# Rotary halves on VectorE, and auxiliary steps of a two-layer decoder kernel put in other places, other banks and other sums

## What is computed

```
h = x + 0.5 * rms_norm(swiglu(rms_norm(x), ffn1))
r_q, r_k, r_v, r_g, g_qkv, g_z, g_a, g_b, m_q, gates = split(rms_norm(h) @ w_in)
rotary:  concat([x1 * cos - x2 * sin, x1 * sin + x2 * cos])      # halves of 128 rows, 4 heads of q and of k
o_ret = silu(r_g) * rms_norm(retention(rotary(r_q), rotary(r_k), r_v))
o_gdn = rms_norm(gated_delta(l2(q), l2(k), v)) * silu(g_z)       # q, k, v = silu(short causal convolution of g_qkv)
o_mem = softmax(m_q @ mem_k) @ mem_v                             # 4 heads over 256 memory rows
merged = sigmoid(gates) * (o_ret @ W_ret, o_gdn @ W_gdn, o_mem @ W_mem), summed
h = h + rms_norm(merged @ w_out);  h = h + 0.5 * rms_norm(swiglu(rms_norm(h), ffn2))
```

## Time and profile before

| | |
|---|---|
| median of 3 runs | 1933.48 us (1932.43 to 1934.76) |
| the profiled execution | 1930.05 us |
| its span | 1928.3 us |
| mean granted TensorE clock | 0.99 |
| VectorE, ScalarE, GpSimd busy | 1349.1, 903.6, 120.2 us |
| DMA | 372.48 MB, 193 GB/s |

### The profile page before, as it was taken

The page is one execution under the profiler, slowest core; times in us unless marked ns, Lnnn a source line. Parts: engine busy times, 40 slices in busy tenths (PEclk is TensorE's granted clock), DMA queues, the critical chain, the costliest instruction groups (busy, mean ns, idle before and its releaser), DMA issues. The chain is left out here.

```text
span 1928.3 us, 40625 instructions
## 1 busy us (share of the span) xinstructions
PE 1849.2 (96%) x16354; PEld 1785.9 (93%) x16354; DVE 1349.1 (70%) x2070; ACT 903.6 (47%) x1048; POOL 120.2 (6%) x176
## 2 busy tenths in 40 slices
PE   6999999999998999999999999999999899999997
PEld 6999999988888999999999999998888899999997
DVE  5777577758666867776577756777676776877755
ACT  3533355456654264533354334464566435353433
POOL 0000001101210100000000000110111010000000
PEclk9999999999999999999999999999999999999998
DMA  7676657666764556565667766665666564556653
GB/s 234 187 204 193 182 178 230 213 218 211 253 208 155 180 177 206 164 183 160 182 196 215 200 177 187 214 227 196 232 232 208 166 194 158 175 187 186 185 163 113
DMA packets 436075, 372.48 MB, mean 193 GB/s; under 512 B 9474, under 2 KB 413316, under 8 KB 435010
## 3 DMA queue, kind: packets, MB, share of 16 engines
q1 hardware_dynamic: 411728, 278.76, 48.5%
q0 software_dynamic: 24160, 91.12, 13.6%
HBM read 343.16 MB, written 26.69 MB: 192 GB/s over the span
## 5 line engine op out<-in xcount | busy, mean ns | idle before, releaser
L1715 DVE TENSOR_TENSOR wl<-raw,wh 128x2048 fp32r<-128x2048 f32 (+1 forms) x282 | 603.7, 2141 | 192.3 <-ACT wh L1261 165.5
L1261 ACT CAST wh<-raw 128x2048 fp32r<-128x2048 f32 (+1 forms) x282 | 503.9, 1787 | 250.2 <-PE proj L652 121.7
L652 PE MATMUL proj<-xl,wh 128*128 128x264 f32 x2624 | 380.8, 286 | 0.5 <-DVEq L1846 0.5
L652 PE MATMUL proj<-xh,wh 128*128 128x264 f32 x2624 | 380.7, 288 | 0.0
L652 PE MATMUL proj<-xh,wl 128*128 128x264 f32 x2624 | 371.1, 284 | 2.1 <-DVE wl L1715 2.1
L652 PEld LDWEIGHTS proj<-xl,wh 128*128 128x128 f32 x2624 | 342.0, 189 | 14.1 <-issue 13.2
L652 PEld LDWEIGHTS proj<-xh,wh 128*128 128x128 f32 x2624 | 341.2, 189 | 1.9
L652 PEld LDWEIGHTS proj<-xh,wl 128*128 128x128 f32 x2624 | 339.1, 188 | 3.4 <-DVE wl L1715 3.4
L671 PE MATMUL proj<-hl,wh 128*128 128x264 f32 x704 | 173.3, 283 | 0.0
L670 PE MATMUL proj<-hh,wh 128*128 128x264 f32 x704 | 173.0, 283 | 0.0
L1282 ACT ACTIVATE gate<-gate 128x264 f32<-128x264 f32 x88 | 37.4, 425 | 248.0 <-DVEq L1747 248.0
(11 more groups left out here) (444 smaller groups left out, 2383.0 us busy)
## 6 DMA issues: line engine op xcount, KB each, us to landing
raw<-ffn_w_in SPq DMA_DIRECT2D x176, 512.0 KB, 5.1
raw<-w_in SPq DMA_DIRECT2D x80, 1024.0 KB, 5.6
raw<-ffn_w_out SPq DMA_DIRECT2D x64, 704.0 KB, 4.6
sring<-cache_mem_k POOLq DMA_DIRECT2D x32, 512.0 KB, 5.0
sring<-cache_mem_v POOLq DMA_DIRECT2D x32, 512.0 KB, 4.4
out<-sring POOLq DMA_DIRECT2D x32, 512.0 KB, 4.3
sring<-state_gdn POOLq DMA_DIRECT2D x32, 512.0 KB, 5.4
raw<-w_mem_v SPq DMA_DIRECT2D x10, 1024.0 KB, 6.3
```

The costliest lines, as they stand in the source:

```text
L652: mm = pe.matmul(o, w[:, s, k * 256 + t * P:k * 256 + (t + 1) * P], a[:, k, :], **go)
L1261: act.copy(wh[:, slot, 0:size], raw[:, slot, 0:size]).then_inc(hi_done[slot], 1)
L1715: dve.tensor_sub(wl[:, slot, 0:size], raw[:, slot, 0:size], wh[:, slot, 0:size].bitcast(F32)).then_inc(split_done[slot], 1)
```

## The change

In both layers:

- The swap products and their table are gone. `rotate` makes the swapped halves itself: two VectorE operations of 64 partitions, each reading the other half's partitions, then cosines and sum; the sign moves in the table.
- gq: `rvn0`, `rvn1` from the ends of groups 0 and 1 to the middle and end of group 3, `ro0`, `ro1` to those of group 4, `rst` to the middle of 5, `rvs` from the end of 4 to the middle of 6, `rqd` to the end of 1, `gcs` from the middle to the end of 5. Banks are fixed by `FIRST_BANK` from here to the delta's decays.
- x2: `svt` is turned inside the first half, `rd0` after it, and VectorE takes them in this order; `gct0`, `gct1` one group later; at the end `rS7` comes first, and VectorE updates the state before it reads `gqd` and `rdt`.
- `gvn1` goes from x2's end to rg's first middle, `gkn` from there to the middle of x0's second group, where ScalarE copies it (before: VectorE, 1.22 us).
- The squares are added in pairs by VectorE (`pair_sums`, three operations), so `rn0`, `rn1`, `gm0`, `gm1` take 2 matmuls each and not 4. `rn` goes from the end of rg's group 0 to the middle of group 1. In the decays of the second chunk `gG1` stands before `gbr1`.

```diff
...
-                def rotate(j):
-                    o = begin(l, f"rw{j}")
-                    for t in range(2):
-                        mm = pe.matmul(o[:, t, 0:T], swap[:], rot[:, 2 * j + t, :], start=True, stop=True)
-                    end(mm, f"rw{j}")
...
                     elif g == 3:
+                        ready("rvt")
+                        turn_values(0)
+                    elif g == 4:
                         ready("rvn")
                         outputs(0)
-                    elif g == 4:
+                    elif g == 5:
                         ready("rkd")
                         o = begin(l, "rst")
...
                         end(mm, "rst")
+                    elif g == 6:
+                        turn(l, "rvs", [(j * P, rvt[:, j, SEQ:T]) for j in range(KT)])
...
+                    elif g == 3:
+                        turn_values(1)
+                    elif g == 4:
+                        outputs(1)
                     elif g == 5:
                         pe.wait_ge(scr_loaded, 16 * (l + 1))
                         turn(l, "gcs", [(j * 24, scr[:, j * P:(j + 1) * P]) for j in range(16)])
...
                     if (t, k) == (0, 3):
...
+                        if g:
+                            state_rows(g)
+                        else:
+                            turn_rows("svt", accv, 1)
...
-                        turn_rows("svt", accv, 1)
+                        state_rows(0)
...
-                    if g == 7:
+                    if g == 6:
+                        turn_delta_values(0)
+                    elif g == 7:
+                        update_retention(8)
                         turn_rows("rdt", accr, 2)
                         ready("gprod")
                         o = begin(l, "gqd")
                         end(pe.matmul(o[:, 0, 0:H * NS], ones[:], kneg[:].rearrange("p h b -> p (h b)"), start=True, stop=True), "gqd")
-                    if g in (6, 7):
-                        turn(l, f"gvn{g - 6}", [(j * P, qkvt[:, 8 + j, (g - 6) * P:(g - 5) * P]) for j in range(KT)])
-                    if g == 7:
-                        update_retention(8)
...
                 def turn_keys(g):
                     if g == 0:
-                        ready("gqk")
-                        turn(l, "gkn", [((2 * h + t) * P, qkvt[:, 4 + h, t * P:(t + 1) * P]) for h in range(H) for t in range(2)])
-
-                def finish_retention(g):
-
-                    if g == 0:
-                        ready("rsq")
+                        turn_delta_values(1)
+                    elif g == 1:
+                        second("rsq", 1)
                         for s in range(2):
                             o = begin(l, f"rn{s}")
                             for hd in range(2):
-                                for dt in range(2):
-                                    mm = pe.matmul(o[:, hd, 0:T], ones[:], rsq[:, 4 * s + 2 * hd + dt, :], start=(dt == 0), stop=(dt == 1))
+                                mm = pe.matmul(o[:, hd, 0:T], ones[:], rsq[:, 2 * s + hd, :], start=True, stop=True)
                             end(mm, f"rn{s}")
...
+                        elif g == 1:
+                            turn(l, "gkn", [((2 * h + t) * P, qkvt[:, 4 + h, t * P:(t + 1) * P]) for h in range(H) for t in range(2)])
...
-                        ready("g2sq")
+                        second("g2sq", 1)
...
                             for hd in range(2):
-                                for dt in range(2):
-                                    mm = pe.matmul(o[:, hd, 0:SEQ], ones[:], sqd[:, 4 * s + 2 * hd + dt, :],
-                                                   start=(dt == 0), stop=(dt == 1))
+                                mm = pe.matmul(o[:, hd, 0:SEQ], ones[:], sqd[:, 2 * s + hd, :], start=True, stop=True)
...
                 def rotate(j):
-                    o = take(dve, l, f"rw{j}")[:, :, 0:T]
                     c = 0 if j < 2 else 2
                     r = rot[:, 2 * j:2 * j + 2, :]
+                    for into, other in ((slice(0, HALF_P), slice(HALF_P, P)), (slice(HALF_P, P), slice(0, HALF_P))):
+                        order.apart(tt(sqt[into], r[other], rot_tab[other, c + 1:c + 2, :].broadcast_to([HALF_P, 2, T]), ALU.mult))
+                    order.wait()
                     order(tt(r, r, rot_tab[:, c:c + 1, :].broadcast_to([P, 2, T]), ALU.mult))
-                    order(tt(sqt[:], o, rot_tab[:, c + 1:c + 2, :].broadcast_to([P, 2, T]), ALU.mult))
-                    release(dve, f"rw{j}")
                     order(tt(r, r, sqt[:], ALU.add))
...
-                    if g < NS:
-                        own_part(accr, take(dve, l, f"rd{g}")[:, 0, 0:DV], own_row, g)
-                        release(dve, f"rd{g}")
                     if g == 0:
                         o = take(dve, l, "svt")[:, 0, :]
...
                         tell("o_mem")
-                    elif g == NS - 1:
+                    if g < NS:
+                        own_part(accr, take(dve, l, f"rd{g}")[:, 0, 0:DV], own_row, g)
+                        release(dve, f"rd{g}")
+                    if g == NS - 1:
                         tell("reads")
...
+                def pair_sums(squares):
+
+                    both = squares[:].rearrange("p (h d) t -> p h d t", d=2)
+                    order(tt(squares[:, 0:1, :], squares[:, 0:1, :], squares[:, 1:2, :], ALU.add))
+                    order(tt(squares[:, 1:2, :], squares[:, 2:3, :], squares[:, 3:4, :], ALU.add))
+                    order(tt(squares[:, 2:4, :], both[:, 2:4, 0, :], both[:, 2:4, 1, :], ALU.add))
+
                 def finish_retention(g):
+                    read_delta(g)
                     if g == 0:
-                        order(cp(kn[:].rearrange("p n d -> p (n d)"), flat("gkn")))
-                        release(dve, "gkn")
-                    read_delta(g)
+                        second("rsq", 0)
+                        pair_sums(rsq)
+                        tell("rsq")
...
```

More of the change, by code:

```diff
@@ L21 @@
 AX = mybir.AxisListType
-P = 128
+P, HALF_P = 128, 64
 L = 2
@@ L102 @@
             + " ".join(f"{n}{s}" for n in ("gG", "gQ") + tuple(f"{n}{g}" for n in ("gy", "gt") for g in range(LEVELS)) for s in range(2)) + " " + " ".join(f"{n}{g}" for n in ("gc", "gu") for g in range(SMALL))).split()
-FIRST_BANK = {"rn0": 2}
+FIRST_BANK = {"rn0": 2, **{n: 0 for n in "rkn rs0 rs1 rvn0 rvn1 ro0 ro1 rst rvs".split()}, **{n: 2 for n in "rqd rks gcs".split()},
+              **{f"sv{g}": 3 for g in range(NS)},
+              "spt": 2, "rd7": 2, "rS6": 0, "rS7": 2, "rdt": 0, "gqd": 1, "gvn1": 2, "gd0": 1, "rn1": 0, "gd1": 2, "gbr0": 0, "gG0": 3, "gQ0": 2,
+              "gd2": 0, "gG1": 1, "gbr1": 2, "gQ1": 0}
 PLACE, AUX_USES, AUX_FULL = {}, [0] * 4, [0] * 4
@@ L149, in build @@
         kdec_tab = sb("kdec_tab", [P, 2 * H])
-        ident, swap, tri, ones = (sb(n, [P, P]) for n in ("ident", "swap", "tri", "ones"))
+        ident, tri, ones = (sb(n, [P, P]) for n in ("ident", "tri", "ones"))
         masks = sb("masks", [P, 7, P])
@@ L937, in retention_middle, with turn_values, retention @@
                         end(mm, "rst")
+                    elif g == 6:
+                        turn(l, "rvs", [(j * P, rvt[:, j, SEQ:T]) for j in range(KT)])
+                def turn_values(t):
+                    turn(l, f"rvn{t}", [(j * P, rvt[:, j, t * P:(t + 1) * P]) for j in range(KT)])
+                def retention(g):
+                    if g == 1:
+                        ready("rprod")
+                        o = begin(l, "rqd")
+                        end(pe.matmul(o[:, 0, 0:H * NS], ones[:], kneg[:].rearrange("p h b -> p (h b)"), start=True, stop=True), "rqd")
+                    elif g == 2:
+                        turn(l, "rks", [(h * P, rot[:, 4 + h, SEQ:T]) for h in range(H)])
+                    elif g == 3:
+                        turn_values(1)
+                    elif g == 4:
+                        outputs(1)
                     elif g == 5:
@@ L940, in retention_middle @@
                         turn(l, "gcs", [(j * 24, scr[:, j * P:(j + 1) * P]) for j in range(16)])
[L942 to L957, removed]
                 products(l, "gq", xh, xl, after=retention, mid=retention_middle, inner=values)
@@ L1036, in decays, with key_products @@
                     mats = [(q, 2 * s + q // 2, q % 2) for q in range(4)]
+                    def key_products(step, other):
+                        o = begin(l, f"{step}{s}")
+                        for q, h, c in mats:
+                            mm = pe.matmul(o[:, 0, q * P:(q + 1) * P], qkvt[:, 4 + h, c * P:(c + 1) * P],
+                                           qkvt[:, other + h, c * P:(c + 1) * P], start=True, stop=True)
+                        end(mm, f"{step}{s}")
+                    if s == 0:
+                        ready("gqk")
+                    else:
+                        key_products("gG", 4)
                     o = begin(l, f"gbr{s}")
```

(8 more changed lines are left out.)

138 lines of the change are left out of this document (70 added, 68 removed).

## The result

| | before | changed |
|---|---|---|
| median, 10 runs each | 1932.95 us (1926.45 to 1935.75) | 1938.68 us (1936.89 to 1942.09) |
| ratio to before, 95% interval | | 1.0045 (1.0034 to 1.0055) |
| profiled execution | 1930.05 us | 1936.89 us |

The account below looks back on a forecast made before the run. TensorE, busy 96% of 1928.3 us, was taken as the bound. Gains less waits and clock summed to 2.7 us in layer 1 and 5.3 in layer 0, 8.0 together: 1933.5 - 8.0 = 1925.5 us, 8-in-10 range 1917 to 1932.

Parts of the forecast that it names:

- Rotary: End of rv: VectorE's rotations bound it, TensorE's removed 3.7 us become waiting; net 0.4 us later per layer.
- The clock's 0.9 per layer: End of rv: the clock may fall behind the rotary stops, costing 0.9 us per layer, bounds 0 and 1.7.
- gq and x2's start: gq: three stops go, one new comes, 1.9 us gained; x2's start: the `o_mem` stop of 1.50 us goes.
- The x2 term of 4.4: x2's start: stops at `o_mem` (1.50) and `gct0` (1.19) and the half clock (1.70) go, per layer.
- x2's end: The 1.16 us stop at `rS7` goes, as it no longer stands behind GpSimd's and VectorE's other work.
- the term of -3.9: x2's end and rg: TensorE reaches the second read of the delta states 3.9 us earlier.
- None of these hangs on what is removed: Second delta state read: GpSimd's chain of stores and loads does not move, so layer 1 gains nothing.
- Term: 3.8: Second delta state read, layer 0: 2.9 us turned into waiting and 0.9 for the clock behind it.
- a wait of 6.1: Second delta state read, layer 1: TensorE's wait for the load grows from 2.24 to 6.1 us.
- The term of -1.1: gz: `gm` loses 4 of 8 matmuls, with some 0.7 us of waiting for pair sums; 1.1 us gained per layer.
- Rival (c): End of rv: half operations crossing partitions cost much more; 1936.7 us if both halves take 1.4; chance 0.08.
- (b): x2's start: `o_mem` stays late as VectorE doesn't catch up; 1931.9 us, or 1934.3 without `gct0`'s gain; chance 0.17.

Follow-up runs that it names:

- e7: Changed kernel with only GpSimd's last retention state store issued before the wait for the store ahead of it; 0.9959 of the kernel before, 1923.70 us.
- e8: Changed kernel with rotary undone, `rd7` in bank 0 and the last state store issued first; 0.9940 of the kernel before.
- e10: Changed kernel, rotary as changed, with `rd7` in bank 0 and the last state store issued first; 0.9960 of the kernel before.

## Why the prediction was wrong

**Rotary.** Right. VectorE is the bound, the removed 3.7 us are waited (though at `sall` and `rkn`, not at `ps` and `rkn`), a rotation takes 2.95, and the part alone costs 2.1 us, with an interval from nothing to 4.4, against a forecast of 2.6 with the clock. The clock's 0.9 per layer were nothing in one layer and 1.3 in the other.

**gq and x2's start.** Right in mechanism, `o_mem` included: its stop is gone. -1.9 and -1.5 against -1.9. The x2 term of 4.4 was 3.1: it took all of the earlier trace rows and the clock of the earlier trace rows as gained, and a small new stop of 0.32 stands ahead of `gn0`. Where the other 1.0 is wasn't traced.

**x2's end: the step that failed first.** "The stop of 1.16 at `rS7` goes" was true, but the prediction went through the new places and not through the new banks. `gvn0` falls in banks 2 and 3 and `FIRST_BANK` puts `rd7` in 2, and ScalarE frees `gvn0` behind a cast of 1.9 us. That is 1.78 and 1.49 us of stop; the term of -3.9 was measured as -2.7 and -2.8. The banks are in the kernel's tables and could have been read before the run.

**The load: the step that cost most.** The sentence "None of these hangs on what is removed" failed. For layer 0 it counted the load as issued when it was before and TensorE as 3.9 earlier; but TensorE had gained 4.6 more in front of this, which the sum booked as a gain and did not carry to the load. It came 7.2 earlier. The chain did move too: the last store was issued 2.7 us earlier (526.93 for 529.63). But the 5.8 us of the store were taken for fixed, and it became 8.6, so the load was issued no earlier than before. In the trace this goes with the weight load issued 0.58 us ahead of the store, where it stood 1.08 behind. Term: 3.8, measured 7.9. For layer 1 the forecast gave a wait of 6.1, measured 5.76, and that is luck: counted from the start of its rv, TensorE came 5.5 us earlier and not 3.9, and the load was issued 1.7 earlier and not at the same time; the two errors cancel. e7 shows that the chain was the cause: with the store first the kernel takes 14.7 us less.

**gz and what is behind it.** The term of -1.1 was measured in its stretch (-1.2, -1.2) and lost in the next: the split there waits for ScalarE and VectorE, which start no earlier. The earlier trace rows look at the wait of TensorE alone, not at who waits behind. The sum put g1, b1 and out at nothing without a reason, and they were 4.8 and 2.6.

With the chain repaired (e7, e8, e10) the kernels come out at 0.994 to 0.996, where the forecast was 0.9959. That is luck as well: the forecast held 3.8 + 6.4 us of wait and clock at the load, which these kernels don't have. Without them it would have been 1915.3, a ratio of 0.9906. The other terms were too good by about this difference, 2.6 us in x2, 2.3 at its end and 7.4 behind gz. Rival (c), at 1936.7 the nearest in time, was no part of it: the half operations took 0.70 us each. Nor was (b): `o_mem` was not late.

What stays open: why g1, b1 and out take 1.4 us more in layer 0 even without the pair sums, and what delays a weight load of b1, for which ScalarE waited 2.60 us in the changed kernel's layer 0 (0.50 before). In all fourteen traces the first stop of out goes with this wait: where it was 0.4 to 0.8, TensorE stopped 1.1 to 1.6 us, and where it was 1.25 to 2.7, 1.7 to 3.1. The long ones are only in kernels with both the rotary on VectorE and the delta pair sums. No experiment changed these loads.

## What to carry to other kernels

When a change brings the bound engine forward, carry the whole lead, not the local one, to the next thing that it does not own: a transfer chain in fixed order takes the lead back, and adds the half clock. Issue a store when its data is made, not behind the wait for the one ahead; it gains only where an engine waits for what follows (14.7 us here, nothing in the kernel before). When steps move, go through the buffers as through the steps: ask for each who filled its bank last and when that reader, on another engine and behind its other work, lets go.

## Of the hardware, unexpected

From its issue to that of the load that waits for it, a 512 KB state store took 5.5 to 6.2 us when issued at least 0.43 us before a 1 MB weight load, and 7.9 to 8.8 when issued after it or less than 0.35 before (16 cases; a regularity, not tested by moving the weight load alone).

Seven waits for the delta load, of 4.2 to 6.05 us, were followed by a granted clock of 0.61 to 0.78 over 8 us, that is, the 1.2 GHz level for 3.5 to 6.2 of them. Behind shorter stops it varied: 1.00 behind the 2.24 us of the earlier trace rows, and, at the same place of one execution, 0.79 behind a stop of 2.23 and 1.00 behind one of 2.24. So a term for the clock behind a stop of about 2 us can be nothing or over 1 us.

And a stop put down to "issue" may be a semaphore wait whose release the profile did not show: regrouping the banks took such stops of 2.12 and 1.97 us away, though part of their time came back later.
